# Feature-major up projections, two activation buffers and modulation sums in pieces

## The chip, the cores and the metric

The kernel runs on one core of one Trainium2 chip. The metric is the device time of one execution in microseconds. The engines are PE (TensorE), DVE (VectorE), ACT (ScalarE), POOL (GpSimd) and SP (SyncE, which here only issues transfers). Each engine works through its own list of instructions in order and meets the others only at semaphores.

## The reference

The kernel computes two transformer blocks of two kinds for 256 tokens of width 1024, all in float32. What the change touches are three feed-forward stages and one set of vector-matrix products:

```
mod = silu(c) @ w_mod[i] + b_mod[i]              # 6 vectors of 1024 for each of two layers
sh1, sc1, g1, sh2, sc2, g2 = split(mod, 6)
h = modulate(rmsnorm(x, norm_mlp[i]), sh2, sc2)
a = relu(h @ w_up[i])                            # 256 x 1024 @ 1024 x 4096, layers 0 and 1
x = x + g2 * ((a * a) @ w_down[i])
...
(silu(x @ w_gate) * (x @ w_up)) @ w_down         # second block, width 2816
```

The second block also has a gated delta rule, an attention with forgetting, and its own projections, none of them changed.

## The kernel before

**Weights.** Every weight matrix goes through `raw`, a ring of four slots of 2 MB that SP fills. A slot becomes one tile `t` of work in three steps. ACT copies it to `wh` in a 32-bit matmul format (line 557), DVE writes what is left of it, `raw - wh`, to `wl` (line 1049), and PE multiplies three times for each product: high with high, high with low, low with high (`PASSES`). `wh` and `wl` hold one tile, in two halves. A half may be overwritten when PE has used it (`split_used`), and PE may start on one when DVE has finished it (`split_l`). `split` makes four quarters of a tile, on ACT and on DVE alike.

**The two MLP stages** (called MLP0 and MLP1 below) have 8 steps each. `up(j)` computes 512 of the 4096 hidden features, `down(j)` multiplies them back into the four open PSUM banks 0 to 3. `up` keeps tokens on the partitions: a matmul has 128 tokens of `H` or `L` (the high and low part of the input) as weights and 512 columns of `wh` or `wl` passing, 48 of them in a tile. The result has tokens on partitions, but `down` needs features there. So ACT takes the ReLU (602), POOL squares it into `act` (452), PE transposes `act` (`turn`, 1646, eight transposes), ACT copies the transposed result from PSUM to `aTh` (607) and DVE takes the low part `aTl` (1083). There is one `aTh` and one `aTl`. PE's order is `up(j)`, `down(j-1)`, `turn(j)`.

**The gated stage** of the second block (FFN below) has 11 steps of 256 features: `g_up`, `g_down` and `g_turn` in the same order, with SiLU on ACT (852) and the product on DVE (1489). A `g_down` tile is half as large.

**Layer 1's modulation vectors** are summed inside MLP0. In each of steps 2 to 7, SP brings two pieces of `w_mod[1]` of 1 MB to slots 0 and 1. DVE multiplies each by `silu(c)` and adds over 8 row blocks (`mod_halves`, lines 933 and 936, 16 instructions in one go) into `acc`. PE sums over the partitions with four matmuls of one column (1723), and DVE adds the bias (`mod_cols1`, 964), which waits for these matmuls. SP refills a slot when `mod_acc` or `mod_accb` says that the sum is made; the last weights of MLP0, `w_down[0][7]`, go to slot 0 and wait for `mod_acc` 17, which is the last sum in that slot. `gate_diag` (993, DVE) and `gate_mm` (1611, PE) then spread the gate vector g2 over the partitions before the last `down`.

**Elsewhere** four tiles of the QKV projection already run feature-major (1749): 128 features as weights, 256 columns of tokens passing, 96 matmuls in a tile.

Of the kernel before, what the change touches and what calls it, by code (L numbers as in the profile page):

```python
# [56 lines left out]
def build(nc, a, out):  # L57
    ctx = ExitStack()
    with ctx:
# [344 lines left out]
        def _(e):  # L404
# [44 lines left out]
            def squares(it):  # L449
                for m in range(NM):  # L450
                    e.wait_ge(S["r_done"], 2 * it + m + 1)
                    e.tensor_tensor(act[:, m, :], relu[:, m, :], relu[:, m, :], ALU.mult).then_inc(S["a_done"], 1)  # L452
            squares(0)
# [79 lines left out]
        def _(e):  # L533
# [62 lines left out]
            def mlp_relu(it, t):  # L596
                for m in range(NM):
                    if m == 0:
                        e.wait_ge(S["u_done"], it + 1)
                    else:  # L600
                        e.wait_ge(S["split_used"], 2 * t + 2)
                    e.activation(relu[:, m, :], ps[:, 4 + m, :], ACT.Relu).then_inc(S["r_done"], 1)  # L602

            def mlp_aT(it):
                for b in range(2):
                    e.wait_ge(S["t_done"], 2 * it + b + 1)
                    e.activation(aTh[:, 2 * b:2 * b + 2, :],
                                 ps[:, 6 + b, :].rearrange("p (k t) -> p k t", k=2), ACT.Copy).then_inc(S["th_done"], 1)

# [1527 lines left out]
```

## Time and profile before

| what | value |
|---|---|
| three runs | 1228.77, 1230.62, 1233.9 us, median 1230.62 |
| the profiled execution's own time (its span) | 1229.1 us |
| PE, DVE, ACT, POOL busy | 89%, 55%, 37%, 9% of the span |
| MLP0, first `up` matmul to the end of the last `down` | 113.9 to 322.6 us |
| MLP1, the same | 515.6 to 711.8 us |
| FFN, the same | 1016.9 to 1218.6 us |

A row of the timeline gives the start, the duration, the engine, the line, the operation, output and inputs, the shape and the count of merged instructions; in brackets the idle time before it and what ended it. The duration of a matmul is longer than the distance to the next, because matmuls overlap; what a stretch of them takes is read from starts. PEclk is the granted TensorE clock: 1.00 is 2.4 GHz, 0.50 is 1.2 GHz.

### The profile page before, as it was taken

How to read it: one execution, taken by the hardware profiler on the slowest of the kernel's cores; microseconds unless marked ns; L12 is line 12 of the kernel's file. 1: busy time of each engine (PE TensorE's matmuls, PEld its weight loads, DVE VectorE, ACT ScalarE, POOL GpSimd, SP SyncE). 2: the span in 40 equal slices, each digit the busy share in tenths (PEclk: the TensorE clock that was granted, in tenths of full speed). 3: DMA queues.
4: the chain of work that ended last, by engine and by line, in shares of the span. 5: the costliest groups of instructions: out<-in, count | busy, mean ns of one | idle time of the engine just before them, and what ended most of it. 6: DMA issues, size and time to landing. Idle time of an engine off the chain costs nothing.

```text
span 1229.1 us, 14350 instructions
## 1 busy us (share of the span) xinstructions
PE 1098.8 (89%) x5513; PEld 927.8 (75%) x5513; DVE 681.5 (55%) x1074; ACT 451.5 (37%) x748; POOL 109.6 (9%) x108
## 2 busy tenths in 40 slices
PE   5489999999799898899999879999869689999995
PEld 5488777777698688678888669986659677777774
DVE  5487666776645894544444366623373545554453
ACT  1113433433444321444444345542222334443342
POOL 2000100101000000010010010001074000000000
PEclk9976999999799657899999869985679988999998
DMA  9876577677354653154454513540000023545510
GB/s 342 286 271 228 211 253 266 208 270 271 140 206 151 206 192 138 71 200 160 185 196 177 188 47 131 203 137 1 1 1 1 19 85 103 183 159 191 185 68 34
DMA packets 105178, 195.47 MB, mean 159 GB/s; under 512 B 2283, under 2 KB 46572, under 8 KB 105132
## 3 DMA queue, kind: packets, MB, share of 16 engines
q1 hardware_dynamic: 104380, 192.58, 44.6%
q0 software_dynamic: 752, 2.26, 0.5%
q8 instruction: 31, 0.51, 0.2%
q14 instruction: 15, 0.12, 0.0%
HBM read 193.76 MB, written 1.07 MB: 159 GB/s over the span
## 4 chain that ended last, share of the span: by engine, by line
PE 70%; DVE 16%; ACT 5%; issue 5%; DMA 3%; POOL 1%; SPq 1%; DVEq 0%; ACTq 0%; POOLq 0%
PE ps L1593 16%; PE ps L1632 12%; PE ps L1661 10%; PE ps L1858 6%; DVE wl L1049 5%; PE ps L1749 4%; DMA raw<-in_w_mod 3%; PE ps L2077 3%; DVE arena L909 2%; PE ps L1543 2%; ACT wh L557 2%; DVE arena L936 2%; PE ps L1993 1%; ACT arena L574 1%; PE ps L1762 1%
## 5 line engine op out<-in xcount | busy, mean ns | idle before, releaser
L1049 DVE TENSOR_TENSOR wl<-raw,wh 128x1024 fp32r<-128x1024 f32 (+1 forms) x288 | 314.0, 1135 | 306.1 <-ACT wh L557 305.8
L557 ACT ACTIVATE wh<-raw 128x1024 fp32r<-128x1024 f32 (+1 forms) x288 | 267.9, 982 | 364.6 <-PE ps L1593 135.1
L1593 PE MATMUL ps<-wh,H 128*128 128x512 f32 x288 | 117.5, 408 | 6.1 <-DVE L L1032 3.3
L1593 PE MATMUL ps<-wl,H 128*128 128x512 f32 x288 | 116.2, 403 | 0.0
L1593 PE MATMUL ps<-wh,L 128*128 128x512 f32 x288 | 115.4, 401 | 0.0
L1661 PE MATMUL ps<-wh,aTh 128*128 128x512 f32 x256 | 103.2, 403 | 8.9 <-DVE wl L1049 8.9
L1632 PE MATMUL ps<-wh,H 128*128 128x512 f32 x256 | 103.4, 404 | 2.4 <-DVE wl L1049 2.4
L1661 PE MATMUL ps<-wl,aTh 128*128 128x512 f32 x256 | 102.7, 401 | 0.0
L1661 PE MATMUL ps<-wh,aTl 128*128 128x512 f32 x256 | 102.5, 400 | 0.0
L1632 PE MATMUL ps<-wl,H 128*128 128x512 f32 x256 | 101.4, 396 | 0.0
L1632 PE MATMUL ps<-wh,L 128*128 128x512 f32 x256 | 101.2, 395 | 0.0
L452 POOL TENSOR_TENSOR arena<-arena 128x512 f32<-128x512 f32 x32 | 45.2, 1428 | 347.7 <-ACT arena L602 347.7
L1593 PEld LDWEIGHTS ps<-wh,H 128*128 128x128 f32 x288 | 55.9, 194 | 22.5 <-DVE wl L1049 5.0
L1593 PEld LDWEIGHTS ps<-wh,L 128*128 128x128 f32 x288 | 55.6, 193 | 13.2
L1661 PEld LDWEIGHTS ps<-wh,aTh 128*128 128x128 f32 x256 | 49.0, 191 | 21.6 <-issue 6.9
L1593 PEld LDWEIGHTS ps<-wl,H 128*128 128x128 f32 x288 | 55.7, 194 | 12.1
L1632 PEld LDWEIGHTS ps<-wh,H 128*128 128x128 f32 x256 | 48.7, 190 | 15.9 <-issue 3.9
L1661 PEld LDWEIGHTS ps<-wh,aTl 128*128 128x128 f32 x256 | 49.0, 191 | 12.1
L1661 PEld LDWEIGHTS ps<-wl,aTh 128*128 128x128 f32 x256 | 49.1, 192 | 11.9
L1632 PEld LDWEIGHTS ps<-wh,L 128*128 128x128 f32 x256 | 48.5, 189 | 11.6
L1858 PE MATMUL ps<-H,wh 128*128 128x272 f32 x192 | 56.8, 296 | 0.3 <-DVE wl L1049 0.3
L1858 PE MATMUL ps<-L,wh 128*128 128x272 f32 x192 | 56.4, 294 | 0.0
(373 smaller groups left out, 1943.2 us busy)
## 6 DMA issues: line engine op xcount, KB each, us to landing
raw<-in_w_up SPq DMA_DIRECT2D x16, 2048.0 KB, 7.5
raw<-in_w_down SPq DMA_DIRECT2D x16, 2048.0 KB, 7.7
raw<-in_w_mod SPq DMA_DIRECT2D x12, 2048.0 KB, 9.7
raw<-in_w_in SPq DMA_DIRECT2D x7, 2048.0 KB, 7.5
raw<-in_w_mod SPq DMA_DIRECT2D x12, 1024.0 KB, 7.5
raw<-in_w_qkv SPq DMA_DIRECT2D x6, 2048.0 KB, 10.9
raw<-in_w_mod SPq DMA_DIRECT2D x8, 1536.0 KB, 7.0
raw<-in_w_gate SPq DMA_DIRECT2D x11, 1024.0 KB, 5.3
```

The costliest lines, as they stand in the source:

```text
L452: e.tensor_tensor(act[:, m, :], relu[:, m, :], relu[:, m, :], ALU.mult).then_inc(S["a_done"], 1)
L557: e.activation(dst, src, ACT.Copy).then_inc(S["split_h"], 1)
L909: ins = e.scalar_tensor_tensor(out=dst, in0=w[:, k, :], scalar=ccol[:, 0, k:k + 1], in1=dst, op0=ALU.mult, op1=ALU.add)
L936: ins = e.scalar_tensor_tensor(out=dst, in0=w[:, k, 0:256], scalar=ccol[:, 0, k:k + 1], in1=dst, op0=ALU.mult, op1=ALU.add)
L1049: e.tensor_tensor(o, src, i1.bitcast(F32), ALU.subtract).then_inc(S["split_l"], 1)
L1543: e.matmul(ps[:, 2, c:c + 1], w[:, k, P * c:P * c + P], ccol[:, 0, k:k + 1], start=(c == 0 and k == 0), stop=False)
L1593: ins = e.matmul(ps[:, bank, :], src[xa][:, 4 * hb + k, META + P * m:META + P * m + P], w[wb][:, k, :], start=(hb == 0 and k == 0 and n == 0),
L1632: ins = e.matmul(ps[:, 4 + m, :], (H, L)[xa][:, 4 * hb + k, META + P * m:META + P * m + P], w[wb][:, k, :], start=(hb == 0 and k == 0 and ...
L1661: ins = e.matmul(ps[:, 2 * m + c, :], (aTh, aTl)[xa][:, 2 * hb + k, P * m:P * m + P], w[wb][:, k, 512 * c:512 * c + 512], start=False, sto ...
L1749: ins = e.matmul(ps[:, b + hb, SEQ * c:SEQ * c + SEQ], w[wb][:, k, P * c:P * c + P], (H, L)[xa][:, k, META:TT], start=(k == 0 and n == 0), ...
L1858: ins = e.matmul(ps[:, b + 2 * hb + c, 0:TT], w[wb][:, k, P * c:P * c + P], (H, L)[xa][:, k, :], start=(k == 0 and n == 0), stop=(k == KD ...
L2077: ins = e.matmul(ps[:, 2 * m + c, :], (aTh, aTl)[xa][:, hb, P * m:P * m + P], (wh, wl)[wb][:, hb, 512 * c:512 * c + 512], start=False, sto ...
```

## The change

All `up` tiles of MLP0, MLP1 and FFN become feature-major (`feature_rows`), with 96 matmuls of 256 columns. The first half of a tile gives features 0 to 255 in PSUM bank 4, the second 256 to 511 in bank 5. `turn` and `g_turn` are gone. ACT writes the ReLU and then squares it straight into `aTh`; POOL squares it too, into `act`; DVE takes `aTl` as `act - aTh`, both of them now in SBUF. There are two of `aTh` and `aTl`. In MLP0 the four modulation matmuls stand between `up(j+1)` and `down(j)`, and the 16 DVE instructions of `mod_halves` are spread over the quarters of the two tiles around them. The second block's step is arranged likewise. SP's part is not touched.

```
-            def mlp_relu(it, t):
-            def mlp_aT(it):
+            def mlp_act(it, buf, t, b, first=False):
+                e.wait_ge(S["split_used"], 2 * t + b + 1)
+                if not first:
+                    e.wait_ge(S["a_done"], 2 * it - 1 + b)
+                r = relu[:, 2 * b:2 * b + 2, :]
+                e.activation(r, ps[:, 4 + b, :].rearrange("p (k t) -> p k t", k=2), ACT.Relu).then_inc(S["r_done"], 1)
+                e.wait_ge(S["r_done"], 2 * it + b + 1)
+                e.activation(aTh[buf][:, 2 * b:2 * b + 2, :], r, ACT.Square).then_inc(S["th_done"], 1)
...
-            with e.Fori(2, 7) as j:
-                split(T_MLP0 + 2 * j, 3)
-                mod_halves(j)
-                split(T_MLP0 + 1 + 2 * j, 2)
+            def mlp0_steps(j, r):
+                split(T_MLP0 + 2 * j, 3, qs=(0, 1))
+                mod_halves(j, r, (0, 1))
+                split(T_MLP0 + 2 * j, 3, qs=(2, 3))
+                mod_halves(j, r, (2, 3))
+                mlp_low(j, r)
+                split(T_MLP0 + 1 + 2 * j, 2, cols=True, qs=(0, 1))
+                mod_halves(j, r, (4, 5))
+                split(T_MLP0 + 1 + 2 * j, 2, cols=True, qs=(2, 3))
+                mod_halves(j, r, (6, 7))
                 mod_cols1(j)
-                mlp_aT(j)
-            mod_halves(7)
+            with e.Fori(1, 3) as i:
+                for r in range(2):
+                    mlp0_steps(2 * i + r, r)
+            mlp0_steps(6, 0)
+            split(T_MLP0 + 14, 3, qs=(0, 1))
+            mod_halves(7, 1, (0, 1, 2))
+            split(T_MLP0 + 14, 3, qs=(2, 3))
+            mlp_low(7, 1)
+            mod_halves(7, 1, (3, 4, 5, 6, 7))
+            split(T_MLP0 + 15, 0)
             nch[0] += 14 * 6
-            split(T_MLP0 + 14, 3)
             gate_diag(modc[:, 0, 40:48])
             mod_cols1(7)
-            mlp_aT(7)
-            split(T_MLP0 + 15, 0)
             gate_copy(1, 4)
...
+            def feature_rows(t, free):
+                for b in range(2):
+                    half(t, b)
+                    if free is not None:
+                        e.wait_ge(free[0], free[1] + (b if len(free) == 3 else 0))
+                    w = [q[:, b, :].rearrange("p (k n) -> p k n", k=KD) for q in (wh, wl)]
+                    for c in range(2):
+                        for k in range(KD):
+                            parts(k)
                             for n, (xa, wb) in enumerate(PASSES):
+                                ins = e.matmul(ps[:, 4 + b, SEQ * c:SEQ * c + SEQ], w[wb][:, k, P * c:P * c + P],
+                                               (H, L)[xa][:, k, META:TT], start=(k == 0 and n == 0),
+                                               stop=(k == KD - 1 and n == 2))
                     ins.then_inc(S["split_used"], 1)
...
             up(0, T_MLP0)
-            turn(0)
             up(1, T_MLP0 + 1)
-            down(0, T_MLP0 + 2)
-            e.wait_ge(S["r_done"], 4)
+            down(0, 0, T_MLP0 + 2)
+            up(2, T_MLP0 + 3)
...
-            turn(1)
-            with e.Fori(2, 8) as j:
-                up(j, T_MLP0 - 1 + 2 * j, 10 + j)
-                down(j - 1, T_MLP0 + 2 * j)
+            down(1, 1, T_MLP0 + 4)
+            with e.Fori(1, 3) as i:
+                for r in range(2):
+                    j = 2 * i + r
+                    up(j + 1, T_MLP0 + 1 + 2 * j)
+                    mods_layer1(j, r)
+                    down(j, r, T_MLP0 + 2 + 2 * j)
+            up(7, T_MLP0 + 13)
+            mods_layer1(6, 0)
+            down(6, 0, T_MLP0 + 14)
+            mods_layer1(7, 1)
             e.wait_ge(S["mod_col"], 18)
+            e.wait_ge(S["r_done"], 16)
             gate_mm(4)
-            down(7, T_MLP0 + 15, last=True)
+            down(7, 1, T_MLP0 + 15, last=True)
...
-            turn(8)
             with e.Fori(0, 3) as i:
                 for r in range(2):
                     up(9 + 2 * i + r, T_MLP1 + 1 + 4 * i + 2 * r)
-                    down(8 + 2 * i + r, T_MLP1 + 2 + 4 * i + 2 * r)
-                    turn(9 + 2 * i + r)
+                    down(8 + 2 * i + r, r, T_MLP1 + 2 + 4 * i + 2 * r)
...
-            g_turn(0)
             with e.Fori(0, 5) as i:
                 for r in range(2):
                     g_up(1 + r + 2 * i, T_FFN + 1 + 2 * r + 4 * i)
-                    g_down(r + 2 * i, T_FFN + 2 + 2 * r + 4 * i)
-                    g_turn(1 + r + 2 * i)
-            g_down(NJ2 - 1, T_FFN + 21, last=True)
+                    g_down(r + 2 * i, r, T_FFN + 2 + 2 * r + 4 * i)
+            g_down(NJ2 - 1, 0, T_FFN + 21, last=True)
```

On PE, the end of MLP0 before: the last rows of `down(6)` (1661), the modulation matmuls of step 7 (1723), `turn(7)` (1646), the gate (1611) and the first row of `down(7)`.

```order
L1661 MATMUL ps<-wl,aTh 128x512
L1661 MATMUL ps<-wh,aTl 128x512
L1723 MATMUL ps<-ones,arena 128x1 [waits mod_accb,mod_acc,r_done]
L1723 MATMUL ps<-ones,arena 128x1 x3
L1646 MATMUL ps<-ident,arena 128x128 [waits tl_done,a_done]
L1646 MATMUL ps<-ident,arena 128x128 x7
L1716 REGISTER_ALU
L1716 COMPARE_AND_BRANCH
L1611 MATMUL ps<-arena,ones 128x128 [waits gate_diag,mod_col]
L1611 MATMUL ps<-arena,ones 128x128 [waits gate_diag] x7
L1661 MATMUL ps<-wh,aTh 128x512 [waits split_l,tl_done]
```

On PE now, one step earlier: the last rows of `up(7)` (1651), the modulation matmuls of step 6 (1732) and the start of `down(6)` (1671).

```order
L1651 MATMUL ps<-H,wh 128x256
L1651 MATMUL ps<-H,wl 128x256
L1651 MATMUL ps<-L,wh 128x256
L1732 MATMUL ps<-ones,arena 128x1 [waits mod_col,mod_accb,mod_acc]
L1732 MATMUL ps<-ones,arena 128x1 x3
L1671 MATMUL ps<-wh,aTh_49 128x512 [waits split_l,tl_done]
```

The modulation matmuls stood between a `down` and a `turn`; they now stand between an `up` and a `down`, and no transposes are behind them.

On DVE, the end of MLP0's loop before and what follows it: the bias of step 6's sums (964, `modc`), `aTl` (1083), the whole of `mod_halves(7)`, the `wl` of `down(6)`, the gate, and the `wl` of `down(7)` (1049 for the second time).

```order
L964 ISA [waits mod_mm]
L964 TENSOR_TENSOR modc<-ps,pcol 128x4
L1083 TENSOR_TENSOR aTl<-ps,aTh 128x512 [waits th_done] x2
L1160 REGISTER_ALU
L1160 COMPARE_AND_BRANCH
L933 TENSOR_SCALAR arena<-raw,ccol 128x256 [waits mod_mm,raw_in0]
L933 TENSOR_SCALAR arena<-raw,ccol 128x256 [waits raw_in1]
L936 SCALAR_TENSOR_TENSOR arena<-raw,ccol,arena 128x256 [waits mod_chain] x14
L1049 TENSOR_TENSOR wl<-raw,wh 128x1024 [waits split_h] x4
L993 TENSOR_SCALAR arena<-ident,modc 128x128 x8
L964 TENSOR_TENSOR modc<-ps,pcol 128x4 [waits mod_mm]
```

On DVE now, from the bias of step 6's sums on.

```order
L964 TENSOR_TENSOR modc<-ps,pcol 128x4 [waits mod_mm]
L1049 TENSOR_TENSOR wl<-raw,wh 128x1024 [waits split_h] x2
L933 TENSOR_SCALAR arena<-raw,ccol 128x256 [waits mod_mm,raw_in0]
L933 TENSOR_SCALAR arena<-raw,ccol 128x256 [waits raw_in1]
L936 SCALAR_TENSOR_TENSOR arena<-raw,ccol,arena 128x256 [waits mod_chain] x4
L1049 TENSOR_TENSOR wl<-raw,wh 128x1024 [waits split_h] x2
L1084 TENSOR_TENSOR aTl_52<-arena,aTh_50 128x512 [waits a_done,th_done] x2
L936 SCALAR_TENSOR_TENSOR arena<-raw,ccol,arena 128x256 [waits mod_chain] x10
L1049 TENSOR_TENSOR wl<-raw,wh 128x1024 [waits split_h] x4
L993 TENSOR_SCALAR arena<-ident,modc 128x128 x8
L964 TENSOR_TENSOR modc<-ps,pcol 128x4 [waits mod_mm]
L1001 COPY gate<-ps 128x512 [waits gate_mm] x2
```

The `wl` of `down(6)` now starts behind the bias that waits for PE's modulation matmuls, the sums of step 7 end later, and the gate stands behind all four quarters of the `wl` of `down(7)`.

## Rows read from the trace of the kernel before

**Rows 1.** The page: the span, and PE's chain by line.
```profile
span 1229.1 us, 14350 instructions
...
PE ps L1593 16%; PE ps L1632 12%; PE ps L1661 10%; PE ps L1858 6%; DVE wl L1049 5%; PE ps L1749 4%; DMA raw<-in_w_mod 3%; PE ps L2077 3%; DVE arena L909 2%; PE ps L1543 2%; ACT wh L557 2%; DVE arena L936 2%; PE ps L1993 1%; ACT arena L574 1%; PE ps L1762 1%
```
**Rows 2.** PE's timeline in MLP1: a down tile, a turn, the next up.
```profile
542.61 0.40 PE L1661 MATMUL ps<-wh,aTh 128*128 128x512 f32 x1
...
553.81 1.03 PE L1646 MATMUL ps<-ident,arena 128*128 128x128 f32 x8
554.60 0.48 PE L1632 MATMUL ps<-wh,H 128*128 128x512 f32 x1
```
**Rows 3.** PE's timeline, QKV: 336 rows of 256 columns lie between these.
```profile
339.15 0.28 PE L1749 MATMUL ps<-H,wh 128*128 128x256 f32 x1
...
378.91 0.40 PE L1593 MATMUL ps<-wh,H 128*128 128x512 f32 x1
```
**Rows 4.** PE's timeline, MLP1: the first and the last turn.
```profile
530.56 1.09 PE L1646 MATMUL ps<-ident,arena 128*128 128x128 f32 x8 [1.80 <-POOL arena L452]
...
698.17 0.76 PE L1661 MATMUL ps<-wh,aTh 128*128 128x512 f32 x1 [4.17 <-DVE wl L1049]
```
**Rows 5.** Stretches of PE: length, busy (instructions), granted clock, DMA share, GB/s.
```profile
290.80:294.20 3.40, 1.77 (x8) 1.00 0.92 311
311.20:314.60 3.40, 3.40 (x9) 0.51 0.99 299
699.00:703.60 4.60, 4.60 (x12) 0.50 0.47 149
1212.40:1215.80 3.40, 3.40 (x10) 0.50 0.00 0
```
**Rows 6.** PE's timeline in FFN: a step's turn, then the last one.
```profile
1048.42 0.60 PE L2066 MATMUL ps<-ident,arena 128*128 128x128 f32 x4
1049.33 0.50 PE L1593 MATMUL ps<-wh,H 128*128 128x512 f32 x1 [0.31 <-DVE wl L1049]
...
1208.07 0.60 PE L2066 MATMUL ps<-ident,arena 128*128 128x128 f32 x4
1211.37 0.47 PE L2077 MATMUL ps<-wh,aTh 128*128 128x512 f32 x1 [2.70 <-DVE wl L1049]
```
**Rows 7.** PE's timeline in MLP0: its start, and one step.
```profile
113.87 0.50 PE L1632 MATMUL ps<-wh,H 128*128 128x512 f32 x1
...
179.05 0.49 PE L1632 MATMUL ps<-wh,H 128*128 128x512 f32 x1 [0.30 <-DVE wl L1049]
...
201.70 1.02 PE L1723 MATMUL ps<-ones,arena 128*128 128x1 f32 x8
...
203.96 0.49 PE L1632 MATMUL ps<-wh,H 128*128 128x512 f32 x1 [0.30 <-DVE wl L1049]
```
**Rows 8.** DVE's timeline in MLP0: the first two sums of a step, then 14 more.
```profile
193.83 2.18 DVE L933 TENSOR_SCALAR arena<-raw,ccol 128x256 f32<-128x256 f32 x2
...
270.68 5.62 DVE L936 SCALAR_TENSOR_TENSOR arena<-raw,ccol,arena 128x256 f32<-128x256 f32 x14
```
**Rows 9.** PE's timeline at the end of MLP0.
```profile
292.43 0.50 PE L1661 MATMUL ps<-wh,aTh 128*128 128x512 f32 x1 [2.34 <-DVE wl L1049]
...
305.45 1.95 PE L1611 MATMUL ps<-arena,ones 128*128 128x128 f32 x16
309.79 0.47 PE L1661 MATMUL ps<-wh,aTh 128*128 128x512 f32 x1 [2.39 <-DVE wl L1049]
```
**Rows 10.** DVE's timeline: the first wl quarter of the last down.
```profile
307.28 1.23 DVE L1049 TENSOR_TENSOR wl<-raw,wh 128x1024 fp32r<-128x1024 f32 x1
```
**Rows 11.** DMA issues from 285 to 295 us: count, KB each, us to landing.
```profile
raw<-in_w_down SPq DMA_DIRECT2D x1, 2048.0 KB, 7.8
```
**Rows 12.** The costliest groups: out<-in count | busy, mean ns | idle before, releaser.
```profile
L452 POOL TENSOR_TENSOR arena<-arena 128x512 f32<-128x512 f32 x32 | 45.2, 1428 | 347.7 <-ACT arena L602 347.7
L993 DVE TENSOR_SCALAR arena<-ident,modc 128x128 f32<-128x128 f32 x24 | 6.6, 345 | 0.0
```

More of the change, by code:

```diff
@@ L447, in _, with squares @@
             residual()
[L449 to L453, printed above, removed]
+            def squares(it, first=False):
+                for b in range(2):
+                    e.wait_ge(S["r_done"], 2 * it + b + 1)
+                    if not first:
+                        e.wait_ge(S["tl_done"], 2 * it - 1 + b)
+                    r = relu[:, 2 * b:2 * b + 2, :]
+                    e.tensor_tensor(act[:, 2 * b:2 * b + 2, :], r, r, ALU.mult).then_inc(S["a_done"], 1)
+            squares(0, first=True)
             with e.Fori(1, 8) as j:
@@ L457, in _ @@
             residual()
-            squares(8)
-            with e.Fori(9, 16) as j:
+            with e.Fori(8, 16) as j:
                 squares(j)
@@ L594, in to_hf @@
                     ins.then_inc(S["hf_done"], 1)
-            def mlp_relu(it, t):
[L597 to L602, printed above, removed]
-            def mlp_aT(it):
[L605 to L608, printed above, removed]
+            def mlp_act(it, buf, t, b, first=False):
+                e.wait_ge(S["split_used"], 2 * t + b + 1)
+                if not first:
+                    e.wait_ge(S["a_done"], 2 * it - 1 + b)
+                r = relu[:, 2 * b:2 * b + 2, :]
+                e.activation(r, ps[:, 4 + b, :].rearrange("p (k t) -> p k t", k=2), ACT.Relu).then_inc(S["r_done"], 1)
+                e.wait_ge(S["r_done"], 2 * it + b + 1)
+                e.activation(aTh[buf][:, 2 * b:2 * b + 2, :], r, ACT.Square).then_inc(S["th_done"], 1)
             stats(0)
@@ L1492, in g_aT, with g_mul @@
[L1492 to L1499 removed]
+            split(T_FFN, N_FFN % R, cols=True, qs=(2, 3))
+            def g_mul(j, t):
+                e.wait_ge(S["gr_done"], j + 1)
+                e.wait_ge(S["split_used"], 2 * t + 2)
+                if not (isinstance(j, int) and j == 0):
+                    e.wait_ge(S["gtl_done"], j)
+                e.tensor_tensor(act[:, 0:2, :], relu[:, 0:2, :], ps[:, 5, :].rearrange("p (k t) -> p k t", k=2), ALU.mult
+                                ).then_inc(S["ga_done"], 1)
@@ L1508, in _ @@
+                    if not (last and r):
+                        split(t + 1, (N_FFN + 3 + 2 * r) % R, cols=True, qs=(2, 3))
             with e.Fori(0, 4) as i:
@@ L1639, in turn @@
-            def turn(it):
-                e.wait_ge(S["a_done"], 2 * it + 2)
-                if not (isinstance(it, int) and it == 0):
-                    e.wait_ge(S["tl_done"], 2 * it)
-                for k in range(4):
-                    for m in range(NM):
-                        ins = e.transpose(ps[:, 6 + k // 2, (k % 2) * SEQ + P * m:(k % 2) * SEQ + P * m + P],
-                                          act[:, m, P * k:P * k + P], ident[:, :])
-                    if k % 2:
-                        ins.then_inc(S["t_done"], 1)
@@ L1653, in down, with up @@
+            def up(it, t):
+                first = isinstance(it, int) and it == 0
+                feature_rows(t, None if first else (S["r_done"], 2 * it - 1, "each half"))
+            def down(it, buf, t, last=False):
                 e.wait_ge(S["tl_done"], 2 * it + 2)
@@ L2052, in g_up, with g_down @@
             def g_up(j, t):
[L2053 to L2070 removed]
+                first = isinstance(j, int) and j == 0
+                feature_rows(t, None if first else (S["ga_done"], j))
+            def g_down(j, buf, t, last=False):
                 e.wait_ge(S["gtl_done"], j + 1)
```

228 lines of the change are left out of this document (97 added, 131 removed).

## The prediction

> **What bounds the kernel now.** I read the page first, for the span and for the chain that ended last [rows 1]: its largest shares are PE's split matmuls of the tiles that the change touches (lines 1593, 1632, 1661, 2077) and PE work elsewhere, so in these stages PE sets the pace and the other engines count only where PE waits for them. Then I read PE's timeline through the three feed-forward stages, since a change that takes work from PE is worth the distances between its starts, and not the durations printed beside them. In MLP1 a down tile of 48 rows takes from 542.61 to 553.81, 11.20 us, and the next up begins 0.79 us later behind eight transposes, without idle time [rows 2]. In MLP0 a step takes 203.96 - 179.05 = 24.91 us, with 2.26 us between the tiles for the modulation matmuls, the transposes and 0.30 us of waiting [rows 7]. In FFN the transposes are followed by another 0.31 us of waiting for a `wl` [rows 6], so there something else is the limit. Last I read the waits at the stages' ends and the granted clock around them [rows 4 to 6, 9].
>
> The sum is made against the profiled span, 1229.1 us; the median of the three runs is 1.5 us above it, and I add that at the end.
>
> **Narrow rows.** An up tile has 96 matmuls of 256 columns instead of 48 of 512. QKV has the very same form: 336 of them take 378.91 - 339.15 = 39.76 us, 0.1183 each [rows 3], 96 take 11.36. That is 0.16 us more than 11.20. The doubled number of weight loads therefore costs almost nothing. 8 + 8 + 11 tiles: +1.3, +1.3, +1.8 us.
>
> **MLP1.** Nothing is put in the place of the transposes, and nothing else on PE waits. Per step ACT squares where it copied, DVE takes the same two differences, both beside 22.5 us of matmuls. Gone are: six turns inside the loop, 6 x 0.79 = 4.7 us [rows 2]; the first turn with its wait for POOL's square, 1.80 + 0.79 = 2.6 us [rows 4]; the last, about 1.0 for the turn and 4.2 of waiting [rows 4], 5.2 us. That last wait was long because ACT copied the transposed result before it made `wh` of the last tile; with two buffers the last down has its weights early. After it the clock stood at half for at least 4.6 us [rows 5], which cost half of that, 2.3 us, and goes too. What is late next is `wh` and `wl` of the next half, some 4 us after the half before is free, within its 5.6 us of matmuls. Sum: -4.7 - 2.6 - 5.2 - 2.3 + 1.3 = -13.5 us.
>
> **FFN.** Inside a step nothing is won. The up tile waits for its first `wl` half, which needs a `wh` half that PE frees in the middle of the short down tile, and that chain (ACT, then DVE) is as long as before: the 0.91 us of turn and wait [rows 6] stay as a wait alone. At the start a turn and its wait go, about 0.9 by the same rows. At the end 1211.37 - 1208.07 = 3.3 us go, since the last down follows directly, and the half clock behind it (3.4 us at 0.50 [rows 5]) gives 1.7 back. Sum: -0.9 - 3.3 - 1.7 + 1.8 = -4.1 us.
>
> **MLP0, the wait that the change adds.** The order on DVE shows that `wl` of `down(j)` stands behind the bias that ends step j's sums (964), which waits for PE's modulation matmuls. On PE these now stand between `up(j+1)` and `down(j)`. So PE finishes the up tile, runs the four matmuls (1.02 us [rows 7]), DVE adds the bias (0.1), and only then makes the two `wl` quarters that `down(j)` wants; from the start of such a pair to PE's first matmul it is 309.79 - 307.28 = 2.51 us [rows 9, 10]. Together 3.6 us, of which PE is idle for 2.6, where the step had 2.26. ACT's `wh` is long there. Before, DVE had made both halves' `wl` ahead of that bias, so it cost nothing. Behind the waiting bias on DVE are just these quarters, then the sums, and for the quarters PE waits.
> Four steps: 4 x (3.6 - 2.3) = +5.4 us. Between `up(7)` and `down(6)`, where PE waited 2.34 [rows 9], 3.6: +1.2. Narrow rows in `up(3)` to `up(7)`: +0.8.
>
> **MLP0, the start.** From the first matmul to that of `up(3)` it was 179.05 - 113.87 = 65.2 us [rows 7]. Now it is three up and two down tiles, 3 x 11.36 + 2 x 11.20 = 56.5, one wait like the above with twice the one-column matmuls, 4.5, and about 1.5 because the first columns want all of `H` and `L` at once and because the sum of section 11 stands between two halves: 62.5. So -2.7 us.
>
> **MLP0, the last down.** Its weights go to slot 0, which is free when the last sum of step 7 in it is made. Those sums came ahead of `down(6)`'s `wl`; now they come in pieces behind it. From the first `wl` quarter of `down(6)`, which is 2.5 us before that tile: two quarters 2.3; two first sums and four more, 2.18 + 4 x 0.40 = 3.8 [rows 8]; two quarters 2.3; two differences 1.3 (I take a quarter's time for the pair); ten more sums less the last, 3.6. That is 13.3, or 10.8 after `down(6)` begins. The transfer takes 7.8 us [rows 11], ACT's first quarter 1.0, DVE's four quarters 4.6, then the gate's eight instructions, 8 x 0.345 = 2.8 [rows 12], and PE's gate 1.95 [rows 9] with 0.3 for the hand-overs: 29.3 us from the start of `down(6)` to that of `down(7)`. It was 309.79 - 292.43 = 17.4 [rows 9]. +11.9 us, and since half the wait is PE idle, +0.6 for a longer stretch at half clock behind it (2.3 against 1.7 [rows 5]). The bounds: +9 if the pieces never wait, +14 if the landing is slowed by the loads issued with it.
>
> **MLP0, the clock.** Two waits of about the same length stand in the trace: after 2.34 us of idling the clock stayed at 2.4 GHz (1.00 from 290.8), and after 2.39 us it fell to 1.2 GHz (0.51 from 311.2) for 3.4 us, which costs 1.7 [rows 5, 9]. In front of the new waits of 2.6 us stands another microsecond of matmuls one column wide, so a fall is more likely than not. I take 1.4 us for each of the five that are followed by PE-bound work (`down(1)` to `down(5)`; behind `down(6)` the next wait hides it): +7.0. The ends are 0 and 5 x 1.7 = 8.5, or 11.5 with 2.3 each.
>
> **The sum.** MLP0: 5.4 + 1.2 + 0.8 - 2.7 + 11.9 + 0.6 + 7.0 = +24.2. With MLP1 and FFN: 24.2 - 13.5 - 4.1 = +6.6, so 1235.7 us of span, 1237 us for a run. What the missing transposes give, the modulation part takes, and more.
>
> **Rivals.**
> 1. *The waits come, the clock holds.* For it speaks the first of the two rows above. Then 7.0 less: -0.4 us, 1230 us.
> 2. *The new waits don't form and the change is faster.* If DVE had the two quarters ready when PE ends the up tile, each of the six waits would shrink to the matmuls themselves, 6 x 2.6 = 15.6 us, and the clock would hold, 7.0: 1237 - 22.6 = 1214 us. It decides at the point where `wl` of `down(j)` starts before `up(j+1)` ends. The order of DVE is against it: a bias that waits for PE stands in front.
> 3. *POOL's squares get in the way.* A square takes 1.43 us [rows 12], and now the second one of a step becomes ready some 2.7 us after the up tile, when DVE is at the second of the two quarters. In rows 8 two first sums take 2.18 us, while 14 others take 0.40 each, which looks like such a wait for POOL. If the square goes first, each of six waits grows by up to 1.4: +8.4, 1245 us. Against it: the quarter should start 0.4 us before the square is ready.
> The Trainium skill (SBUF: State Buffer, section "Who interferes with whom") says that a DVE instruction with two SBUF inputs contends with a GpSimd instruction that reads SBUF, and that whoever comes first blocks the other for the whole instruction. By it the `wl` quarters and the new form of the `aTl` differences both contend, the old form, with one input in PSUM, did not; it decides nothing by itself, the order of arrival does, and the sum by it would be that of rival 3 or mine.
>
> **How the numbers follow.** The measurement tells about 0.5% from no change, here 1224.5 to 1236.8 us. My forecast 0.58, rival 1 0.17, rival 2 0.09, rival 3 0.16. The forecast's own range is 1232 to 1242, so a little over half of it counts as slower: slower 0.31 + 0.16 = 0.47, same 0.27 + 0.15 = 0.42, faster 0.09 + 0.02 = 0.11. The range reaches down over rival 1, with some 2 us for the terms that I read from single rows, and up to rival 3: 1227 to 1245.
>
> **What would show it.** In MLP0, PE's rows 1732 followed by about 2.6 us of idling ended by DVE's `wl`, six times, and a step of about 26.3 us, or 27.7 with the clock falling; some 17 us between the end of `down(6)` and the start of `down(7)`, with 3 us of small matmuls in them; in MLP1 a step of 22.6 us and no idle time between tiles; in FFN a step of 17.9 us and a wait of about 0.9. It would be wrong if the wait before `down(j)` is ended by something other than DVE's `wl`, if MLP1's ups are slower than QKV's rows say, or if the last load is issued much earlier than 10 us into `down(6)`.

## The result, and the profile after

The changed kernel takes 1242.61 us (median of 4 runs, 1240.24 to 1245.45), the kernel before 1231.22 us beside it (4 runs, 1228.77 to 1233.9). The ratio is 1.0107, with a 95% interval of 1.0067 to 1.0147: slower by about 1%. The forecast was 1237 us with a range of 1227 to 1245; it missed the median by 5.6 us, and 1242.61 lies just above the 1232 to 1242 that it called its own. In span, +6.6 us was said and +10.4 came. Of the 43 runs of the kernel before that stand beside the kernels of this study, six took 1220.5 to 1221.7 us and the others 1225.0 to 1233.9; no trace of a short one was kept, so what makes it stays open.

The page of the changed kernel, the rows that answer to [rows 1, 12]:

```profile
span 1239.5 us, 16633 instructions
...
PE ps L1651 25%; PE ps L1671 13%; PE ps L1874 6%; DVE wl L1049 5%; PE ps L1614 5%; PE ps L1768 4%; PE ps L2079 3%; DMA raw<-in_w_mod 2%; PE ps L1564 2%; DVE arena L909 1%; ACT wh L559 1%; PE ps L2009 1%; ACT arena L576 1%; PE ps L1781 1%; PE ps L1806 1%
...
L455 POOL TENSOR_TENSOR arena<-arena 128x512 f32<-128x512 f32 x32 | 51.4, 1605 | 345.4 <-ACT arena L604 345.4
```

The chain still runs through PE's split matmuls, now in the narrow form (1651). The page doesn't say where 10.4 us of span were lost. For that I cut PE's timeline at each feed-forward stage's first matmul and at the end of its last down tile, for every kernel run here (us of span, from the profiled executions):

| kernel | span | MLP0 | to MLP1 | MLP1 | to FFN | FFN |
|---|---|---|---|---|---|---|
| before | 1229.1 | 208.9 | 192.9 | 196.6 | 304.7 | 201.9 |
| changed | 1239.5 | 234.1 | 190.3 | 182.3 | 308.7 | 199.6 |
| mlp0_old | 1214.7 | 207.8 | 191.1 | 182.4 | 308.9 | 199.8 |
| bias_late | 1214.1 | 208.0 | 190.4 | 182.3 | 308.8 | 199.6 |
| sums_whole | 1220.5 | 212.0 | 193.1 | 182.3 | 308.7 | 199.5 |
| last_load | 1233.5 | 227.8 | 190.6 | 182.4 | 308.8 | 199.5 |
| warm | 1234.6 | 228.1 | 190.7 | 182.4 | 308.8 | 199.6 |
| ffn_free | 1241.7 | 236.7 | 190.7 | 182.4 | 308.8 | 198.5 |
| best | 1199.3 | 194.4 | 190.7 | 182.4 | 308.8 | 198.5 |
| pool_later | 1230.3 | 234.8 | 190.5 | 182.3 | 299.2 | 199.2 |
| best2 | 1191.3 | 194.4 | 193.0 | 182.3 | 299.0 | 198.2 |
| after_again | 1239.4 | 233.9 | 190.5 | 182.4 | 308.7 | 199.5 |

A stage ends here where its last row ends, 0.2 to 0.4 us later than in the table of the kernel before. By the unrounded times MLP0 gives 25.2 us away, MLP1 and FFN bring 14.2 and 2.3, and two stretches that the change doesn't touch move by -2.5 and +4.0.

One step of MLP0 on PE of the changed kernel (start, duration, what, in brackets the idle time before it and what ended it), with the first of the waits ahead; it answers to [rows 7]:

```profile
166.87 0.77 PE L1671 MATMUL ps<-wh,aTh 128*128 128x512 f32 x1 [4.09 <-DVE wl L1049]
...
179.70 0.28 PE L1651 MATMUL ps<-H,wh 128*128 128x256 f32 x1
...
191.03 0.95 PE L1732 MATMUL ps<-ones,arena 128*128 128x1 f32 x8
194.73 0.79 PE L1671 MATMUL ps<-wh,aTh 128*128 128x512 f32 x1 [2.75 <-DVE wl L1049]
...
207.32 0.28 PE L1651 MATMUL ps<-H,wh 128*128 128x256 f32 x1
```

And DVE in the same step, then POOL:

```profile
192.16 0.16 DVE L964 TENSOR_TENSOR modc<-ps,pcol 128x4 f32 x1 [7.23 <-PE ps L1732]
192.32 2.36 DVE L1049 TENSOR_TENSOR wl<-raw,wh 128x1024 fp32r<-128x1024 f32 x2
194.60 1.39 DVE L933 TENSOR_SCALAR arena<-raw,ccol 128x256 f32<-128x256 f32 x2
```
```profile
188.20 1.04 POOL L455 TENSOR_TENSOR arena<-arena 128x512 f32<-128x512 f32 x1 [22.56 <-ACT arena L604]
193.85 1.72 POOL L455 TENSOR_TENSOR arena<-arena 128x512 f32<-128x512 f32 x1 [4.61 <-ACT arena L604]
```

Read them together. DVE stood idle for 7.23 us in front of a bias of 0.16 us that waits for PE's row 1732, and the two `wl` quarters that PE needs next stood behind it. PE then idled 2.75 us, until both were made (192.32 + 2.36 = 194.68). A DVE that idles for PE just before PE idles for DVE is the sign that the order is at fault and not the work. The other waits before down tiles in MLP0 were 3.05, 2.73, 2.78 and 2.61 us. POOL's square that met the `wl` took 1.72 instead of 1.04 us (1.49 to 2.01 in the five like it), while DVE's quarter kept its time (mean 1135 ns before, 1138 after).

Behind the waits, stretches of PE (length, busy, granted clock); the last of the three lies in MLP1's last down tile:

```profile
194.70:198.10 3.40, 3.37 (x9) 0.57 0.89 327
...
222.60:226.00 3.40, 3.35 (x8) 0.50 0.81 296
...
709.00:713.60 4.60, 4.60 (x22) 1.00 0.00 0
```

After each new wait PE ran at about half clock (1.2 GHz; 0.50 to 0.61 over the first 3.4 us, six times), and MLP1's end, which was at 0.50 [rows 5], now has the full 2.4 GHz.

The end of MLP0 on PE, the issue of the last load on SP, and DVE:

```profile
307.18 0.76 PE L1671 MATMUL ps<-wh,aTh 128*128 128x512 f32 x1 [2.61 <-DVE wl L1049]
...
332.40 3.79 PE L1632 MATMUL ps<-arena,ones 128*128 128x128 f32 x16 [11.60 <-DVE modc L964]
335.83 0.78 PE L1671 MATMUL ps<-wh,aTh 128*128 128x512 f32 x1
```
```profile
316.99 0.38 SPq L266 DMA_DIRECT2D raw<-in_w_down  x1
```
```profile
313.32 4.04 DVE L936 SCALAR_TENSOR_TENSOR arena<-raw,ccol,arena 128x256 f32<-128x256 f32 x10
326.07 4.63 DVE L1049 TENSOR_TENSOR wl<-raw,wh 128x1024 fp32r<-128x1024 f32 x4 [8.71 <-ACT wh L559]
330.62 1.65 DVE L993 TENSOR_SCALAR arena<-ident,modc 128x128 f32<-128x128 f32 x8
```

`down(7)` starts 28.65 us after `down(6)`, against 17.36 before [rows 9]. The load of its weights was issued at 316.99, when the ten sums in DVE's first row were nearly done, and DVE then waited 8.71 us for ACT's `wh`.

MLP1's steps and FFN's, on PE, which answer to [rows 2, 4, 6]:

```profile
596.71 0.28 PE L1651 MATMUL ps<-H,wh 128*128 128x256 f32 x1
...
619.24 0.28 PE L1651 MATMUL ps<-H,wh 128*128 128x256 f32 x1
...
1043.89 0.38 PE L1651 MATMUL ps<-H,wh 128*128 128x256 f32 x1 [0.85 <-DVE arena L1506]
...
1061.93 0.38 PE L1651 MATMUL ps<-H,wh 128*128 128x256 f32 x1 [0.82 <-DVE wl L1049]
...
1079.95 0.38 PE L1651 MATMUL ps<-H,wh 128*128 128x256 f32 x1 [0.82 <-DVE wl L1049]
```

A step of MLP1 is 22.53 us and never idle; one of FFN is 18.02 to 18.04 us with 0.82 us of waiting.

### The profile page after: what moved, and what is told of

It is laid out like the page before. It is cut to its first block, busy times and chain, and to the rows that moved or that the text cites. A ratio compares the mean times of both kernels' runs of the same rounds, so it can differ in the third digit from the quotient of the medians.

```text
span 1239.5 us, 16633 instructions
## 1 busy us (share of the span) xinstructions
PE 1088.8 (88%) x6637; PEld 977.7 (79%) x6637; DVE 687.4 (55%) x1063; ACT 455.5 (37%) x737; POOL 111.7 (9%) x108
## 4 chain that ended last, share of the span: by engine, by line
PE 74%; DVE 14%; ACT 4%; DMA 3%; issue 3%; POOL 1%; SPq 1%; DVEq 0%; ACTq 0%; POOLq 0%
PE ps L1651 25%; PE ps L1671 13%; PE ps L1874 6%; DVE wl L1049 5%; PE ps L1614 5%; PE ps L1768 4%; PE ps L2079 3%; DMA raw<-in_w_mod 2%; PE ps L1564 2%; DVE arena L909 1%; ACT wh L559 1%; PE ps L2009 1%; ACT arena L576 1%; PE ps L1781 1%; PE ps L1806 1%
## 5 line engine op out<-in xcount | busy, mean ns | idle before, releaser
L1049 DVE TENSOR_TENSOR wl<-raw,wh 128x1024 fp32r<-128x1024 f32 (+1 forms) x288 | 315.4, 1138 | 291.4 <-ACT wh L559 291.4
L1651 PE MATMUL ps<-H,wh 128*128 128x256 f32 x864 | 245.6, 284 | 10.0 <-DVE wl L1049 7.9
L1651 PE MATMUL ps<-H,wl 128*128 128x256 f32 x864 | 244.7, 283 | 0.0
L1651 PE MATMUL ps<-L,wh 128*128 128x256 f32 x864 | 244.3, 283 | 0.0
L1651 PEld LDWEIGHTS ps<-H,wh 128*128 128x128 f32 x864 | 165.0, 191 | 17.7 <-issue 14.5
L1651 PEld LDWEIGHTS ps<-L,wh 128*128 128x128 f32 x864 | 165.2, 191 | 0.0
L1651 PEld LDWEIGHTS ps<-H,wl 128*128 128x128 f32 x864 | 164.3, 190 | 0.5
L1874 PE MATMUL ps<-H,wl 128*128 128x272 f32 x192 | 56.3, 293 | 0.0
L1564 PE MATMUL ps<-ccol,raw 128*128 128x1 f32 x208 | 40.5, 327 | 14.8 <-DVE modc L920 14.8
L1564 PEld LDWEIGHTS ps<-ccol,raw 128*128 128x128 f32 x208 | 40.4, 299 | 16.4 <-issue 16.4
L1614 PE MATMUL ps<-wh,H 128*128 128x512 f32 x112 | 45.7, 408 | 2.7 <-DVE L L1032 2.7
```

The lines of the kernel that those rows point to most:

```text
L1049: e.tensor_tensor(o, src, i1.bitcast(F32), ALU.subtract).then_inc(S["split_l"], 1)
L1564: e.matmul(ps[:, 2, c:c + 1], w[:, k, P * c:P * c + P], ccol[:, 0, k:k + 1], start=(c == 0 and k == 0), stop=False)
L1614: ins = e.matmul(ps[:, bank, :], src[xa][:, 4 * hb + k, META + P * m:META + P * m + P], w[wb][:, k, :], start=(hb == 0 and k == 0 and n == 0),
L1651: ins = e.matmul(ps[:, 4 + b, SEQ * c:SEQ * c + SEQ], w[wb][:, k, P * c:P * c + P], (H, L)[xa][:, k, META:TT], start=(k == 0 and n == 0), ...
L1874: ins = e.matmul(ps[:, b + 2 * hb + c, 0:TT], w[wb][:, k, P * c:P * c + P], (H, L)[xa][:, k, :], start=(k == 0 and n == 0), stop=(k == KD ...
```

## The experiments

The first four ran together on one chip (the kernel before beside them 1228.25 us), the next four together on the same chip (1228.81), the last two on another (1229.13). Diffs are against the changed kernel, and `...` marks what is left out.

**bias_late.** DVE makes the first two `wl` quarters of the next down tile ahead of the bias that waits for PE.

```diff
-                split(T_MLP0 + 2 * j, 3, qs=(0, 1))
                 mod_halves(j, r, (0, 1))
...
                 mod_halves(j, r, (6, 7))
+                split(T_MLP0 + 2 * j + 2, 3, qs=(0, 1))
                 mod_cols1(j)
```

> The changed kernel with one edit on VectorE: the first two wl quarters of down(j) come ahead of the bias that waits for PE's modulation matmuls, in all six steps; the sums stay in pieces and the last load stays late. Theory A (the bias in front of the quarters makes PE wait, and that wait lets the clock fall): the gap between up(j+1) and down(j) goes from 3.7 us to about 1, the clock stays at 2.4 GHz in these steps, the last down starts some 2.3 us earlier in relation to up(7): 4.1 + 4 x 2.75 + 2.3 = 17.4 us of waits and 8.9 us of half clock, so about 1216 us. Rival B (the pieces of the sums, spread over VectorE, are what costs): the wait stays at 2 us or more, 1238 to 1243 us. Rival C (only the waits, the clock would fall anyway): 1225 us.

Measured: 1215.81 us, ratio 0.9902 (0.9883 to 0.992). PE's timeline where the wait had been:

```profile
186.30 0.95 PE L1732 MATMUL ps<-ones,arena 128*128 128x1 f32 x8
187.11 0.48 PE L1671 MATMUL ps<-wh,aTh 128*128 128x512 f32 x1
...
198.40 0.28 PE L1651 MATMUL ps<-H,wh 128*128 128x256 f32 x1
...
221.82 0.28 PE L1651 MATMUL ps<-H,wh 128*128 128x256 f32 x1
```

The wait and the half clock behind it are gone, a step is 23.42 us instead of 27.62 to 29.20, and MLP0 is 26.1 us shorter. That is theory A (1216 us). The end isn't helped: from `down(6)` to `down(7)` it is 29.57 us here (28.65 in the changed kernel). The place of one instruction of 0.16 us decided whether this change is faster or slower than before.

**last_load.** The last down tile's weights go to slot 2, free early, and one QKV weight goes to slot 0 in their stead.

```diff
-            e.wait_ge(S["mod_acc"], 17)
-            load(0, dview(0), wdn[0][7])
+            free_split(T_MLP0 + 13)
+            load(2, dview(2), wdn[0][7])
```

> The changed kernel with the last w_down of MLP0 loaded to the slot that up(7) leaves free, instead of slot 0 which waits for the last sum; a QKV load takes slot 0 in its place. Theory A (of the 16 us between down(6) and down(7), the late load is the larger part): the load lands long before, the last down waits only for the sums, the quarters and the gate, and starts about 8.5 us earlier, 1233 us, the five waits and clock falls being unchanged. Rival B (VectorE's queue of sums, quarters and gate sets the start anyway, the landing is hidden): less than 3 us, 1240 us.

Measured: 1235.91 us, ratio 1.006 (1.004 to 1.008). PE at MLP0's end:

```profile
308.02 0.77 PE L1675 MATMUL ps<-wh,aTh 128*128 128x512 f32 x1 [2.61 <-DVE wl L1053]
...
326.07 3.78 PE L1636 MATMUL ps<-arena,ones 128*128 128x128 f32 x16 [4.39 <-DVE modc L968]
329.50 0.77 PE L1675 MATMUL ps<-wh,aTh 128*128 128x512 f32 x1
```

From `down(6)` to `down(7)` it is 21.48 us, 7.2 less. What is left of the wait, 4.39 us, is DVE's and ACT's own work for the tile and the gate; the late slot cost the rest.

**warm.** Twenty matmuls of 256 columns, whose result is thrown away, fill the wait before `down(2)` to `down(5)`.

```diff
                     mods_layer1(j, r)
+                    keep_busy()
                     down(j, r, T_MLP0 + 2 + 2 * j)
```

> The changed kernel with 20 matmuls more (256 columns, into a PSUM bank that nobody reads in this stage, the result is thrown away) between the modulation matmuls and down(2) to down(5). They take 2.4 us and fit into PE's wait of 2.7 to 3.0. Theory A (these waits cost a second time by letting the clock fall): the clock stays up in the four steps, 7 us less, 1235.5 us. Rival B (the clock does not matter, or one-column matmuls and idle time are not what lowers it): 1242 to 1244 us.

Measured: 1236.08 us, ratio 1.0055 (1.0036 to 1.0073). PE in one step, then the stretch behind it:

```profile
193.34 2.60 PE L1738 MATMUL ps<-H 128*128 128x256 f32 x20
196.23 0.50 PE L1671 MATMUL ps<-wh,aTh 128*128 128x512 f32 x1 [0.29 <-DVE wl L1049]
...
207.54 0.28 PE L1651 MATMUL ps<-H,wh 128*128 128x256 f32 x1
...
234.17 0.28 PE L1651 MATMUL ps<-H,wh 128*128 128x256 f32 x1
```
```profile
194.50:197.90 3.40, 3.11 (x20) 1.00 1.05 386
```

With PE busy and just as late, the clock stays at 2.4 GHz and the steps take 26.63 and 26.30 us. The four steps take 26.34, 26.63, 26.30 and 26.37 us here and 27.62, 29.20, 27.85 and 27.92 in the changed kernel. So a wait costs its idle time and, apart from it, 1.3 to 2.6 us for the clock behind it, 7.0 for the four. MLP0 as a whole is 6.0 us shorter, since its start, which the edit doesn't touch, took 0.8 longer in this trace.

**best.** bias_late and last_load together; the gate's diagonals are made right after the gate's bias, ahead of MLP0's loop, and the sums of step 7 are divided to suit; and in FFN only the second half of an up tile waits for the product that reads its bank.

```diff
             e.tensor_tensor(modc[:, 0, 40:48], ps[:, 6, 0:8], pcol[:, 0, 40:48], ALU.add).then_inc(S["mod_col"], 2)
+            e.wait_ge(S["mod_col"], 12)
+            gate_diag(modc[:, 0, 40:48])
...
-            e.wait_ge(S["mod_col"], 18)
...
-                feature_rows(t, None if first else (S["ga_done"], j))
+                feature_rows(t, None if first else (S["gr_done"], j), None if first else (S["ga_done"], j))
```

> bias_late and last_load together, with the gate's diagonal made early, the last difference and the last sums in another order, the gate's matmuls no longer waiting for the last bias, and the second half of a g_up alone waiting for the product. Theory A: the waits and falls of bias_late (15.1 + 8.9 us), the last down 16.9 us earlier after up(7), 0.8 of clock behind it, 1.2 in FFN: 42.9 us, so 1200 us. Rival B (something else then limits MLP0, such as the two pieces of w_mod landing late or DVE's total of work): 1210 us or more, with idle time on PE ended by DMA or by DVE's quarters.

Measured: 1202.04 us, ratio 0.9785 (0.9769 to 0.9802). PE at MLP0's end:

```profile
294.54 0.95 PE L1740 MATMUL ps<-ones,arena 128*128 128x1 f32 x8
295.34 2.03 PE L1638 MATMUL ps<-arena,ones 128*128 128x128 f32 x16
297.13 0.48 PE L1679 MATMUL ps<-wh,aTh 128*128 128x512 f32 x1
```

The time is 2 us above what was expected. The wait of 11.60 us is gone, and the gate's matmuls, no longer behind an idle PE, take 2.03 us instead of 3.79. MLP0 is 39.7 us shorter than in the changed kernel. What each of the edits joined here is worth beyond bias_late, last_load and ffn_free wasn't measured.

**mlp0_old.** MLP0 as before the change, MLP1 and FFN as after it.

```diff
-            squares(0, first=True)
...
+            squares_t(0)
...
-                split(T_MLP0 + 2 * j, 3, qs=(0, 1))
-                mod_halves(j, r, (0, 1))
+                split(T_MLP0 + 2 * j, 3)
+                mod_halves(j)
```

> MLP0 as in the kernel before (512-column up tiles, transposes, one activation buffer, the sums of a step in one piece, the last load after the gate's order of before), MLP1 and FFN as changed. By my theory the three parts are independent: MLP1 is worth -14.2 us and FFN -2.4 us by the two traces, so about 16.6 us less than the kernel before of the same chip (ratio about 0.9865), some 1213 us where the kernel before has 1230; MLP0's part of the change alone would then cost 26 to 28 us. Rival (the stages trade with each other, through the throttle: what MLP1 gains is partly given back in the stages behind it, +4.0 us between MLP1 and FFN in the changed kernel's trace): only about 12 us less, 1218.

Measured: 1217.21 us, ratio 0.9916 (0.989 to 0.9941), 11.6 us under the kernel before, so the number of the rival. But its reason holds for a small part only. MLP1 and FFN keep -14.1 and -2.1, and what is given back are 4.2 us between them. About 2.7 of them lie where PE waits for DVE (pool_later), and 1.2 in a stretch further on in which the granted clock is 0.57 here (954 to 958 us) and in the changed kernel (979 to 983), and 1.00 in the kernel before (968 to 972). The second vanished with the first in pool_later, so it was not tested by itself. The end of MLP0, the same code as before, shows how little decides the clock: after 2.38 us of idling in front of `down(7)` it stays at 1.00 here, where it fell to 0.51 after 2.39 us [rows 5, 9], and that tile takes 1.5 us less.

**sums_whole.** bias_late, but the sums of a step in one piece.

```diff
-                mod_halves(j, r, (0, 1))
-                split(T_MLP0 + 2 * j, 3, qs=(2, 3))
-                mod_halves(j, r, (2, 3))
+                mod_halves(j, r, range(KD))
```

> The order of bias_late (the first two wl quarters of the next down ahead of the bias), but the modulation sums of a step are made in one piece of 16 instructions at its head instead of four pieces between the wl quarters. Theory A (DVE has room enough ahead of an up tile's wl, but the pieces are what lets its first half come in time): the wl of each up tile starts about 4 us later, a wait of some 0.8 us forms at up's first half in each of five steps, 4 us over bias_late, ratio about 0.994. Rival B (the pieces don't matter once the bias is out of the way): within 1.5 us of bias_late, ratio 0.990. Rival C (the wait is 2 us or more and the clock falls after it): over 15 us above bias_late, ratio 1.00 or more.

Measured: 1222.06 us, ratio 0.996 (0.9937 to 0.9982). PE's up tiles in it:

```profile
200.33 0.38 PE L1649 MATMUL ps<-H,wh 128*128 128x256 f32 x1 [0.73 <-DVE wl L1049]
...
224.77 0.38 PE L1649 MATMUL ps<-H,wh 128*128 128x256 f32 x1 [0.73 <-DVE wl L1049]
```

MLP0 is 4.0 us longer than in bias_late, as theory A has it: the pieces are worth 4 us (with them the edit moves `aTl` behind the up tile's `wl`), the place of the bias 26. The other 2.7 us lie behind MLP0, and they are the clock's too. The attention's output tile takes 24.05 us instead of 22.48: the granted clock fell to 0.58 there, here and in the kernel before, and stayed at 1.00 in the changed one, behind some 1.94 us of idling in each. Another 1.4 us lie just ahead of it, in transposes and the gate's matmuls, where the clock came back to 1.00 later in the kernels in which it then fell (0.65 from 473 to 476 us in the kernel before, 1.00 from 498.7 to 500.3 in the changed one). The QKV tiles give 0.3 back. best2 is the third kernel with both losses; the other nine have neither. Three rows of stretches there: the kernel before, the changed one, sums_whole.

```profile
482.00:486.00 4.00, 4.00 (x12) 0.58 0.00 0
```
```profile
506.40:510.40 4.00, 4.00 (x19) 1.00 0.00 0
```
```profile
486.00:490.00 4.00, 4.00 (x13) 0.58 0.00 0
```

**ffn_free.** Of best, the edit in FFN alone.

```diff
-                    if free is not None:
+                    if b and free1 is not None:
+                        e.wait_ge(*free1)
+                    elif free is not None:
```

> The changed kernel, except that in FFN the first half of an up tile may overwrite its PSUM bank as soon as the gate's Silu has read it, and only the second half waits for the product that reads the other bank. Theory: the wait of 0.85 us at up(1) goes (it is for the product), the steps in the loop keep their 18.0 us because the 0.82 us there is a wait for wl: about 1 us less than the changed kernel, ratio 1.009. Rival (the product's wait also holds up the loop's steps, hidden behind wl): nine steps of up to 0.8 us, about 7 us less, ratio 1.004.

Measured: 1242.26 us, ratio 1.0114 (1.007 to 1.0157), too wide to see a microsecond (after_again, beside it, took 1241.57). Its trace shows it: FFN takes 198.5 instead of 199.6 us, the wait of 0.85 us at `up(1)` is gone, and the steps keep their 0.82 us for `wl`, so the rival is refuted. MLP0, whose code is the same, took 2.6 us longer in this profile, so single traces differ there by that much.

**after_again.** The changed kernel once more.

> The changed kernel without an edit, beside the others on the same chip, so that their differences from it can be taken there. Every theory: 1.0107 of the kernel before, within 0.3%, a gap before each of down(1) to down(5) of 2.6 to 4.1 us with half clock behind it.

Measured: 1241.57 us, ratio 1.0126 (1.0079 to 1.0173), span 1239.4. Each stage is within 0.2 us of the first profile.

**pool_later.** In the gated-delta stage between MLP1 and FFN, POOL's products wait for DVE's first four.

```diff
             e.wait_ge(S["coef_d"], 3)
+            e.wait_ge(S["sc_d"], 4)
             for m in range(NM):
                 e.tensor_tensor(R1[:, m], v_t[:, m], bc(beta[:, 1 + m, :], P, P), ALU.mult).then_inc(S["sc_p"], 1)
```

What it rests on, DVE and POOL at that place, first in the kernel before:

```profile
892.05 1.05 DVE L1386 TENSOR_TENSOR coef<-nrm,beta 128x12 f32<-128x12 f32 x1 [0.16 <-DVE nrm L1382]
...
894.84 1.53 DVE L1396 TENSOR_TENSOR Kb<-k_t,coef 128x512 f32<-128x512 f32 x1
```
```profile
892.04 2.05 POOL L491 TENSOR_TENSOR DL<-gate,gdec 128x512 f32<-128x512 f32 x2 [55.65 <-DVE nrm L1382]
```

and in the changed one (DVE, PE, POOL):

```profile
900.87 0.17 DVE L1401 TENSOR_TENSOR coef<-nrm,beta 128x12 f32<-128x12 f32 x1
...
903.52 6.75 DVE L1411 TENSOR_TENSOR Kb<-k_t,coef 128x512 f32<-128x512 f32 x1
```
```profile
910.33 1.11 PE L1971 MATMUL ps<-ident,Kb 128*128 128x128 f32 x4 [3.03 <-DVE Kb L1411]
```
```profile
900.98 2.06 POOL L493 TENSOR_TENSOR DL<-gate,gdec 128x512 f32<-128x512 f32 x2 [55.91 <-DVE nrm L1397]
...
903.71 2.02 POOL L501 TENSOR_TENSOR arena<-v_t,beta 128x512 f32<-128x512 f32 x2
...
908.69 1.03 POOL L506 TENSOR_TENSOR arena<-k_t,coef 128x512 f32<-128x512 f32 x1
```

Before, DVE's first product came 0.01 us behind POOL's and waited for it; now it comes 0.11 us ahead. Five instructions later DVE takes 6.75 us for one that takes 0.67 alone, while six of POOL's run back to back from 903.71 to 909.7, and PE waits 3.03 us for it. `Kb` takes 6.75 to 6.77 us in all nine kernels above whose MLP1 is changed.

> The changed kernel, and in the gated-delta stage, which the change doesn't touch, POOL's eight products (R1, Kd and the like) wait until DVE has made its first four (Kn, Kb, Qn, Qg). In the kernel before DVE's Kb took 1.53 us there and POOL's instructions alternated with it; in every kernel with the changed MLP1 Kb takes 6.75 us while six of POOL's run back to back, and the stretch between MLP1 and FFN is 308.7 instead of 304.7 us long. Theory A (the 4 us are only DVE losing the order of arrival to POOL at that place): with the wait Kb takes 0.7 to 1.5 us and the stretch 303 to 305 us, so 4 to 5 us less than the changed kernel, 1237, ratio about 1.008. Rival B (POOL's products are needed soon themselves, and are now 2.5 us later): Kb is short, but PE waits as long for POOL, within 1 us of the changed kernel, 1.012. Rival C (the 4 us are the clock's): the stretch stays at 308.7.

Measured: 1231.93 us, ratio 1.0029 (1.0012 to 1.0046), about twice the gain expected. DVE, then POOL:

```profile
904.40 0.78 DVE L1412 TENSOR_TENSOR Kb<-k_t,coef 128x512 f32<-128x512 f32 x1
```
```profile
906.55 5.20 POOL L502 TENSOR_TENSOR arena<-v_t,beta 128x512 f32<-128x512 f32 x2 [1.93 <-DVE Qg L1412]
```

The stretch is 299.2 us, 9.5 shorter than in the changed kernel and 5.5 shorter than in the kernel before: A, and the kernel before had been paying there too. Some 8.5 of the 9.5 us are won by the time PE starts the matmuls behind these products (914.31 us, 921.94 in the changed kernel). PE's matmuls around there also ran at half clock longer in the changed kernel (0.50 from 910 to 918 us, here 1.00 from 911 to 918), so the 8.5 us are the waits for DVE and the clock behind them together. Now POOL is the one kept out (5.20 us for two that take 2.02). No engine idles for these products, but DVE waits 2.70 instead of 2.16 us for a later one of POOL's (`Al`).

**best2.** best with that wait.

> The kernel best (bias behind the wl quarters, the last load in a slot that is free early, the gate early, the first half of FFN's up tiles free early) with the same wait of POOL. By A: the span 1199.3 becomes about 1195, the median 1198, ratio 0.975. By B or C no change against best, 0.9785.

Measured: 1192.1 us, ratio 0.9693 (0.9671 to 0.9715), span 1191.3. The stretch is 299.0 us, as in pool_later; 2.3 us of it went back in the attention's output tile and just ahead of it (193.0 against 190.7), as in sums_whole. It is the fastest version here, 3% under the kernel before.

## Why the prediction came out as it did

The mechanism was right: MLP0's new wait and its late last load outweigh MLP1's and FFN's transposes, by the order on DVE. That MLP0's sum came out within 1.0 us (+25.2, said +24.2) is partly luck: its start and its four steps cost 1.9 and 1.3 us more than said, its end 2.1 less. Point by point:

- **Narrow rows: right.** MLP1's step is 22.53 us, said 22.6.
- **MLP1: right.** -14.2 us, said -13.5. No tile waits, the half clock at the end is gone.
- **MLP0's wait: right.** Idle 2.6 said; 2.61 to 3.05 measured from `down(2)` on. The four steps take 112.59 us, 12.9 more than before [rows 7]; said 11.6, of which +5.4 for the waits, +0.6 for their narrow rows and +5.6 for the clock. By warm 7.0 are the clock's, which leaves 6.0 for the first two, as said. bias_late shows the cause.
- **The clock: right in kind, a little small.** It fell after every wait. warm's steps put three falls at 1.3, 1.6 and 1.5 us and the one in the step of 29.20 us at 2.6 (half clock for longer: 0.66 from 226.0 to 229.4 us, where the others were at 0.89 or more again); 1.7 on average, said 1.4.
- **MLP0's start: wrong by 1.9.** From the first matmul to `up(3)` 65.77 us, said 62.5 and 1.4 for the clock. The wait at `down(1)` was 4.09 us where I had 2.6 as for the others.
- **The last down: right in length, not in its parts.** 28.65 us, said 29.3. Two errors nearly cancel: the load was issued 9.8 us into `down(6)`, said 10.8, and the gate's matmuls, for which I took 1.95 us from a warm PE, needed 3.79 behind 11.60 us of idling. The clock came back early in `down(7)` (0.50 in the 3.4 us before it, 0.74 in the 3.4 behind), so the 0.6 us there didn't come: that tile took 12.2 us to the stage's end instead of 13.0.
- **FFN: mis-sized.** -2.3, said -4.1. The larger part is the steps: nine of them went from 17.74 to 18.04 us, +0.30 each where I had only the +0.16 of the narrow rows, 1.3 us in all. So the chain that I took to be as long as before had grown by 0.1 to 0.2 us. At the start 0.3 us went where 0.7 was said (0.9 less the narrow rows), since `up(1)` waits 0.85 us for the product (1506), a wait that I had not seen; ffn_free takes it away. The end came as said (4.7 us, said 4.8).
- **The unchanged stretches: missing.** I gave them nothing. They made -2.5 and +4.0 us. Of the second, 2.7 us arise where DVE and POOL meet in another order of arrival, which pool_later shows, and 1.2 in a fall of the clock further on. That the order turns on the 0.12 us shift, and why the shift comes with MLP1's change, was not tested. Of the first, 1.6 us are a fall of the clock in the attention's output tile that was there before and isn't now, and 1.4 are a clock that now comes back earlier ahead of that tile; the QKV tiles take 0.4 us more. What decides these stays open too.
- **Rivals.** The clock holding (1230) is refuted by the half clock behind each wait, the waits not forming (1214) by the rows above; bias_late, whose waits don't form, came out near it. Rival 3 was wrong in its direction: ahead of `down(2)` to `down(6)` DVE's quarters came first each time, and POOL's square stretched to between 1.49 and 2.01 us. The Trainium skill (SBUF — State Buffer, section "Who interferes with whom") says that the order of issue, not the kind of operation, decides who blocks. The trace agrees in MLP0 (1.04 against 1.72 us) and in the gated-delta stage with both signs. The Trainium skill puts the block at one whole instruction, in the same section, and says so of DVE's two-port modes. Here one of DVE's, a product with two inputs in SBUF, took 6.75 us over six of POOL's instructions back to back, which is more than it says.

The miss of 5.6 us in these terms: MLP0 +1.0, FFN +1.8, MLP1 -0.7, the untouched stretches between the stages +1.5 and outside them +0.2, 1.6 between span and median, which are 3.1 us apart where I added 1.5, and 0.2 by which 1237.2 was rounded down.

## What to carry to other kernels

When work leaves an engine, look at what the reordering puts behind an instruction that waits. An instruction of 0.16 us, standing ahead of the weights that PE needs next, cost 26 us in six places; moving it made a loss of 1% a gain of 1%. Where an engine idles for its supplier, and the supplier had just idled for it, change the order first. And compare every stretch between two traces, the untouched ones too: 9.5 us of this study lay in code that nobody had changed. Last, a sum that comes out within 1 us can hide terms that are off by 2; check them one by one.

## What the runs showed of the hardware

- One of DVE and POOL can be held up beside a whole run of the other's instructions, and not beside one only: 6.75 us for DVE's product that takes 0.67, and 5.20 us for two of POOL's that take 2.02. It went with a shift of 0.12 us in who came first.
- The length of PE's idling alone didn't decide the clock. Some 1.94 us in front of the same tile were followed by 0.57 or 0.58 in three kernels (before, sums_whole, best2; the tile took 24.0 us) and by 1.00 in the changed one and in best (22.5 us, as in the seven others); 2.39 us by 0.51 in the kernel before and 2.38 us by 1.00 in mlp0_old, in the same code. After each of the six waits of 2.61 to 4.09 us in the changed kernel's MLP0 it fell.
